# A fused two-block transformer kernel: the pooling stage's bias and banks, a sibling's opening, and products in four gaps

## The reference

```python
for i in range(2):
    f = swiglu(rms_norm(x, g[0]), ffn_w_gate[i, 0], ffn_w_up[i, 0], ffn_w_down[i, 0])   # ffn00, ffn10
    x = x + 0.5 * rms_norm(f, g[1])
    h = rms_norm(x, g[2])
    m = pool_mixer(h, ...) if i == 0 else nsa_mixer(h, ...)                              # pool, nsa
    x = x + rms_norm(m, g[3])
    f = swiglu(rms_norm(x, g[4]), ffn_w_gate[i, 1], ffn_w_up[i, 1], ffn_w_down[i, 1])   # ffn01, ffn11
    x = x + 0.5 * rms_norm(f, g[5])

def pool_mixer(h, w_grp, b_grp, scale):      # group g: trailing mean over 2, 4, 8, 16 tokens minus self
    d = stack([mean_g(h) - h for each of 4 groups of 256 columns])
    return (einsum('bsgc,gce->bsge', d, w_grp) + b_grp).reshape(B, S, D) * scale
```

## Time and profile before

| | |
|---|---|
| time before, median of 3 runs | 2128.64 us (2126.76 to 2135.26) |
| the profiled execution's own time | 2128.28 us |
| its span in the trace | 2126.5 us |
| PE busy | 2050.9 us, 96% of the span |
| DVE busy | 874.7 us, 41% |
| ACT busy | 694.9 us, 33% |
| mean granted TensorE clock | 0.984 of full speed |

### The profile page before, as it was taken

One profiled execution on the slowest core, in us unless ns is written; L12 is line 12 of the kernel. 1 busy time (PEld: TensorE's weight loads), 2 busy tenths in 40 slices (PEclk: granted clock), 3 DMA queues, 4 the chain that ended last, 5 costly groups with the idle time before them and its releaser, 6 DMA issues.

```text
span 2126.5 us, 29241 instructions
## 1 busy us (share of the span) xinstructions
PE 2050.9 (96%) x12345; PEld 1446.3 (68%) x12345; DVE 874.7 (41%) x1244; ACT 694.9 (33%) x966; POOL 16.4 (1%) x30
## 2 busy tenths in 40 slices
PE   8999999999899999999998999899999999899998
PEld 7854444443497444443446999699989988657997
DVE  5831111111376111111116555655575565565555
ACT  5521111111353111111114333433353353454333
POOL 2000000000000000000000000000000000000000
PEclk9999999999999999999999999999999999799999
DMA  8589999999848999999999534545356334505620
GB/s 272 231 374 428 427 429 429 429 429 428 340 159 353 380 427 429 429 429 428 428 428 390 196 127 173 201 155 194 141 216 227 102 129 159 198 1 198 238 99 20
DMA packets 117424, 599.10 MB, mean 282 GB/s; under 512 B 6283, under 2 KB 21867, under 8 KB 92764
## 3 DMA queue, kind: packets, MB, share of 16 engines
q1 hardware_dynamic: 115186, 592.01, 69.5%
q0 software_dynamic: 1888, 5.78, 1.0%
q10 hardware_dynamic: 266, 0.08, 0.0%
HBM read 596.81 MB, written 1.05 MB: 281 GB/s over the span
## 4 chain that ended last, share of the span: by engine, by line
PE 83%; DMA 11%; DVE 4%; ACT 1%; issue 1%; DVEq 0%; ACTq 0%
PE PS L1167 21%; PE PS L1008 16%; PE PS L1181 9%; PE PS L1021 8%; DMA ring<-in_w_expert_up 6%; DMA work<-in_w_expert_up 5%; PE PS L995 4%; PE PS L854 3%; PE PS L1301 2%; PE PS L1154 2%; PE PS L1031 2%; PE PS L906 2%; PE PS L1193 2%; PE PS L1471 1%; PE PS L1048 1%; PE PS L1394 1%
## 5 line engine op out<-in xcount | busy, mean ns | idle before, releaser
L1503 ACT ACTIVATE split<-ring 128x2048 fp32r<-128x2048 f32 x132 | 253.1, 1920 | 410.6 <-PE PS L1167 270.4
L2056 DVE TENSOR_TENSOR split<-ring,split 128x2048 fp32r<-128x2048 f32 x132 | 302.7, 2293 | 170.8 <-ACT split L1503 165.8
L1167 PE MATMUL PS<-hT_high,split 128*128 128x256 f32 x2560 | 329.1, 281 | 0.0
L1167 PEld LDWEIGHTS PS<-hT_high,split 128*128 128x128 f32 x2560 | 316.5, 189 | 2.8
L1008 PE MATMUL PS<-ring,xs 128*64 128x512 f32 x1344 | 301.8, 604 | 12.9 <-DMA ring<-in_w_expert_up 12.9
L1008 PEld LDWEIGHTS PS<-ring,xs 128*64 128x64 f32 x1344 | 99.0, 139 | 209.7 <-issue 198.2
L1021 PE MATMUL PS<-ring,work 128*64 128x512 f32 x672 | 226.6, 595 | 0.0
L1181 PE MATMUL PS<-split,ffn_hid 128*128 128x512 f32 x864 | 202.6, 390 | 0.0
L2319 DVE TENSOR_TENSOR work<-PS,work 128x512 f32<-128x512 f32 x32 | 22.1, 692 | 396.0 <-PE PS L1008 396.0
L1181 PEld LDWEIGHTS PS<-split,ffn_hid 128*128 128x128 f32 x864 | 159.7, 188 | 31.7
L1167 PE MATMUL PS<-hT_low,split 128*128 128x256 f32 x1280 | 178.3, 282 | 0.0
(11 more groups left out here) (333 smaller groups left out, 2140.0 us busy)
## 6 DMA issues: line engine op xcount, KB each, us to landing
ring<-in_w_expert_gate SPq DMA_DIRECT2D x44, 2048.0 KB, 26.0
ring<-in_w_expert_down SPq DMA_DIRECT2D x42, 2048.0 KB, 29.3
ring<-in_w_expert_up SPq DMA_DIRECT2D x40, 2048.0 KB, 26.0
work<-in_w_expert_up SPq DMA_DIRECT2D x24, 2048.0 KB, 26.0
work<-in_w_expert_down SPq DMA_DIRECT2D x22, 2048.0 KB, 27.1
work<-in_w_expert_gate SPq DMA_DIRECT2D x20, 2048.0 KB, 26.4
ring<-in_ffn_w_gate SPq DMA_DIRECT2D x20, 2048.0 KB, 8.7
ring<-in_ffn_w_up SPq DMA_DIRECT2D x20, 2048.0 KB, 9.3
```

The source lines that it names most:

```text
L1167: last = pe.matmul(PS[:, bank, ft * SEQ:(ft + 1) * SEQ], split_cols(b, kind, part)[:, k, ft * P:(ft + 1) * P], hx[:, k, :], start=(n_ == 0 ...
L1503: return act.activation(o, i, ACT.Copy)
L2056: v.tensor_tensor(at[:, 1], src, at[:, 0], ALU.subtract).then_inc(S.w_low, 1)
```

## The change

Three things are changed; the numbers of lines are those of the kernel before.

1. **Pool.** The products of h go into banks 4 to 7 and are taken from there. Right behind them, and ahead of PE's wait for ACT and DVE, four products of one row and 512 columns write the bias into banks 0 to 3 and open them. The eight bias products of 256 columns are gone, and all 16 weight products add to the opened banks.
2. **ffn00's opening.** PE makes the first pass of the up sums between the second and the third pass of the gate sums, and spreads the norm factor behind all 96 products. ACT takes its half of the transposes between its two squares of the raw x, and makes two high parts (up of block 0, gate of block 1) ahead of the squares of the scaled x. DVE makes `hT_low` ahead of scaling x, and the low part of up of block 0 ahead of the norm factor and the diagonal.
3. **Gap products.** In `transpose_x`, between the transposes of token tile 0 and the wait for tile 1, there are 13 filler products in ffn01 and 7 in ffn10, nsa and ffn11, into bank 0.

The other feed-forward stages keep their order: `first_sums` is only written in another way there.

```diff
@@ transpose_x
                         if t and k % 2:
                             last.then_inc(S.hT_psum, 1)
+                    if t == 0 and name in ("ffn01", "ffn10", "nsa", "ffn11"):
+                        keep_clock(13 if name == "ffn01" else 7)
@@ ffn, PE
+                def first_sums():
+
+                    pe.wait_ge(S.w_low, w.to(S.w_low))
+                    one_pass("gate", 0, hT_high, first=True)
+                    one_pass("gate", 1, hT_high)
+                    if name == "ffn00":
+                        pe.wait_ge(S.w_high, w.to(S.w_high, 2))
+                        one_pass("up", 0, hT_high, first=True)
+                        pe.wait_ge(S.hT_low, w.to(S.hT_low))
+                        one_pass("gate", 0, hT_low, last_part=True)
                     else:
+                        pe.wait_ge(S.hT_low, w.to(S.hT_low))
+                        one_pass("gate", 0, hT_low, last_part=True)
+                        spread_r()
                         pe.wait_ge(S.w_high, w.to(S.w_high, 2))
...
+                        one_pass("up", 0, hT_high, first=True)
+                    one_pass("up", 0, hT_low)
+                    pe.wait_ge(S.w_low, w.to(S.w_low))
+                    one_pass("up", 1, hT_high, last_part=True)
+                    if name == "ffn00":
+                        spread_r()
@@ pool_mix, PE
-                        last = pe.matmul(PS[:, c // 2, (c % 2) * SEQ:(c % 2 + 1) * SEQ], hp[:, t, c * P:(c + 1) * P],
+                        last = pe.matmul(PS[:, 4 + c // 2, (c % 2) * SEQ:(c % 2 + 1) * SEQ], hp[:, t, c * P:(c + 1) * P],
                                          means[:, t, c // 2, :], start=(t == 0), stop=(t == 1))
                     if c % 2:
                         last.then_inc(S.hT_psum, 1)
+                for j in range(2 * TT):
+                    pe.matmul(PS[:, j, :], ones[0:1, 0:P], bias[:, (j % 2) * 512:(j % 2 + 1) * 512],
+                              start=True, stop=False, skip_group_check=True)
...
                         for c in range(2):
-                            pe.matmul(o, hT[:, 2 * g + c, t * P:(t + 1) * P], wv[:, 2 * g + c, :],
-                                      start=(c == 0), stop=False)
-                        last = pe.matmul(o, ones[0:1, 0:P], bias[:, g * 256:(g + 1) * 256],
-                                         start=False, stop=True)
+                            last = pe.matmul(o, hT[:, 2 * g + c, t * P:(t + 1) * P], wv[:, 2 * g + c, :],
+                                             start=False, stop=(c == 1), skip_group_check=True)
@@ final, ACT
                     act.wait_ge(S.act_step, w.to(S.act_step))
+                    if t == 0:
+                        take_ffn_hT(FFN_GAIN["ffn00"])
                 roots(root, ss, D, S.root_ready)
-                take_ffn_hT(FFN_GAIN["ffn00"])
+                high("ffn00", 0, "up")
+                high("ffn00", 1, "gate")
...
                 roots(rootc, ssc, D, S.root_ready)
-                high("ffn00", 0, "up")
@@ ffn, DVE
                 w.past(S.hT_odd, 2)
+                v.wait_ge(S.hT_odd, w.after(S.hT_odd, 0))
+                v.wait_ge(S.hT_even, w.after(S.hT_odd, 0))
+                for k in range(KT):
+                    last = v.scalar_tensor_tensor(hT_low[:, k, :], PS[:, 4 + k // 2, (k % 2) * SEQ:(k % 2 + 1) * SEQ],
+                                                  gT[:, gain, k:k + 1], hT_high[:, k, :], ALU.mult, ALU.subtract)
+                last.then_inc(S.hT_low, 1)
                 if name == "ffn00":
                     final_gain = gain_rows()
...
-                v.wait_ge(S.hT_odd, w.after(S.hT_odd, 0))
...
-                last.then_inc(S.hT_low, 1)
+                    low(name, 0, "up")
...
-                low(name, 0, "up")
+                if name != "ffn00":
+                    low(name, 0, "up")
```

More of the change, by code:

```diff
@@ L787, in transpose_h, with keep_clock @@
                 pe.wait_ge(S.hT_odd, w.to(S.hT_odd, 2))
+            def keep_clock(n_, bank=0):
+                for _ in range(n_):
+                    pe.matmul(PS[:, bank, :].rearrange("p (s k) -> p s k", s=4), ident_r[:, :],
+                              ident_r[:, :].unsqueeze(1).to_broadcast([P, 4, P]), start=True, stop=True)
             def transpose_x(name, bank):
@@ L1085, in experts @@
                 return past_more
-            def keep_clock(n_, bank=0):
-                for _ in range(n_):
-                    pe.matmul(PS[:, bank, :].rearrange("p (s k) -> p s k", s=4), ident_r[:, :],
-                              ident_r[:, :].unsqueeze(1).to_broadcast([P, 4, P]), start=True, stop=True)
             def moe(l):
@@ L1135, in split_cols, with one_pass @@
                     return split[:, buffer_of(b, kind), part, :].rearrange("p (k n) -> p k n", k=KT)
-                def first_sums(kind):
-                    gate = kind == "gate"
-                    if gate:
-                        pe.wait_ge(S.w_low, w.to(S.w_low))
-                    else:
+                def one_pass(kind, part, hx, first=False, last_part=False):
+                    for k in range(KT):
+                        if kind == "gate" and first and k % 2 == 0:
+                            odd = (k // 2) % 2
+                            pe.wait_ge(S.hT_odd if odd else S.hT_even, w.to(S.hT_odd if odd else S.hT_even))
+                        for ft in range(2):
+                            last = pe.matmul(PS[:, 2 * (kind == "up") + ft, 0:SEQ],
+                                             split_cols(0, kind, part)[:, k, ft * P:(ft + 1) * P], hx[:, k, :],
+                                             start=(first and k == 0), stop=(last_part and k == KT - 1))
+                    if last_part:
+                        last.then_inc(S.ffn_used, 1)
@@ L1143, in first_sums @@
                         pe.wait_ge(S.w_high, w.to(S.w_high, 2))
-                    for n_, (part, hx) in enumerate(products() if gate else ((0, hT_high), (0, hT_low), (1, hT_high))):
-                        if gate and n_ == 2:
-                            pe.wait_ge(S.hT_low, w.to(S.hT_low))
-                        if not gate and n_ == 2:
-                            pe.wait_ge(S.w_low, w.to(S.w_low))
-                        for k in range(KT):
-                            if gate and n_ == 0 and k % 2 == 0:
-                                odd = (k // 2) % 2
-                                pe.wait_ge(S.hT_odd if odd else S.hT_even, w.to(S.hT_odd if odd else S.hT_even))
-                            for ft in range(2):
-                                last = pe.matmul(PS[:, 2 * (kind == "up") + ft, 0:SEQ],
-                                                 split_cols(0, kind, part)[:, k, ft * P:(ft + 1) * P], hx[:, k, :],
-                                                 start=(n_ == 0 and k == 0), stop=(n_ == 2 and k == KT - 1))
@@ L1211, in ffn @@
                 transpose_x(name, 4)
-                first_sums("gate")
-                pe.wait_ge(S.diag_made, w.to(S.diag_made))
-                for t in range(TT):
-                    last = pe.matmul(PS[:, 4, t * P:(t + 1) * P], ones, FB.sF[:, t, 0:P], start=True, stop=True)
-                last.then_inc(S.r_wide, 1)
-                first_sums("up")
+                first_sums()
                 wide_sums(1, "gate")
@@ L1794, in follow @@
                     high(name, b, "down")
-                high(name, 1, "gate")
+                if name != "ffn00":
+                    high(name, 1, "gate")
                 follow(0)
@@ L2463, in ffn @@
                     w.past(S.x_ready, TT)
-                v.wait_ge(S.hT_odd, w.after(S.hT_odd, 0))
-                v.wait_ge(S.hT_even, w.after(S.hT_odd, 0))
-                for k in range(KT):
-                    last = v.scalar_tensor_tensor(hT_low[:, k, :], PS[:, 4 + k // 2, (k % 2) * SEQ:(k % 2 + 1) * SEQ],
-                                                  gT[:, gain, k:k + 1], hT_high[:, k, :], ALU.mult, ALU.subtract)
-                last.then_inc(S.hT_low, 1)
+                    low(name, 0, "up")
                 v.wait_ge(S.root_ready, w.to(S.root_ready))
```

12 lines of the change are left out of this document (9 added, 3 removed).

## The result

| | median | runs | lowest to highest |
|---|---|---|---|
| before | 2131.75 us | 20 | 2124.81 to 2135.31 |
| after | 2123.48 us | 20 | 2118.09 to 2129.08 |

The ratio is 0.9972, with a 95% interval of 0.9965 to 0.9979. That is 6.0 us less, between 4.5 and 7.5, where I had forecast 9.4 (0.9955). The two medians of the table lie 8.3 us apart and the means 7.0; I go by the ratio on record, which has the interval. The change is well clear of zero and under the 0.5% bound. The profiled execution after took 2122.55 us with a span of 2120.8, against 2128.28 and 2126.5.

The account below looks back on a forecast made before the run. PE was taken as the bound from ffn00 on, through idle time, slow-clock products and products that can be left out. 2.4 + 3.0 + 4.0 = 9.4 us gave 2119.0 us, ratio 0.9955, range 2112.5 to 2125.

Parts of the forecast that it names:

- ffn00, 2.4 us forecast: ffn00's opening: reordered work lets block 1 start at 1153.6 in place of 1156.02; gain 2.4 us, bounds 1.9 and 2.9.
- The gap products, 4.0 us forecast: Fillers keep the clock full behind four gaps: 1.65 (ffn01), 0.8 (ffn10), 0.55 (ffn11), 1.0 us (nsa); bounds 0 and 4.6.
- The pool, 3.0 us forecast: Pool: bias products in one piece ahead, DVE's two tile chains without a hole; gain 3.0 us, bounds 2.4 and 3.3.
- rival B: Pool: one-row bias openings lower the clock, tile 0 comes 1.7 to 3.4 us later; 2120.7 to 2122.4 us; chance 0.09.
- The switches: Pool: two switches between 128 rows and one cost 0.4 us per group; afterwards one at either end of the bias products.
- rival A: The clock inside nsa falls elsewhere: down to 2114 to 2117 us, chance 0.18; up to 2122 to 2123, chance 0.14.
- My own sign of being wrong: In nsa: a change of its length by more than 2 us would show the prediction wrong.
- rival C: The gap products do not hold the clock, only 2.4 + 3.0 us remain: 2123.2 us; chance 0.07.

Follow-up runs that it names:

- openings of 128 rows: The changed kernel with its four openings made with 128 rows instead of one, columns of the matrix of means in place of the bias; ratio to before 0.9960.
- fillers ahead of h: The changed kernel with 16 filler products added in PE's idle time ahead of h; one time, 2123.58 us.
- pool alone: The kernel before with only the pool's part of the change (banks, four wide one-row openings, weight products adding to them); ratio to before 0.9999.
- early openings: The changed kernel with its one-row openings moved into PE's idle time ahead of h, in two pairs; ratio to before 0.9956.

## Why the prediction was wrong in the pool, and where it was right

- **ffn00, 2.4 us forecast, 2.46 measured.** Right by its own steps: DVE's work was permuted without a hole, its low part of gate 1 is the releaser, and no new wait came behind. In four more kernels it was 2.48.
- **The gap products, 4.0 us forecast.** 1.70, 0.87 and 0.61 in the three feed-forward stages, and in nsa the product behind its first 48 starts 12.43 us after the second transposes in place of 13.50, 1.07: together 4.25. DVE's hT_low took the bound over with a wait of 0.2 us, as I had it. But the 4.0 was priced from one execution, in which the clock happened to be slow behind all four gaps. Over the three profiles without fillers the mean is 2.0 us, and the kernel with the fillers alone gained 2.3 (-0.2 to 4.7). That the term came out between these two traces is in part luck.
- **The pool, 3.0 us forecast, 1.7 lost (+4.10 and -2.38).** This is the step that failed: "16 weight products stream in 6.8 us, and the four bias products ... in 3.4 us", all at the full clock. That DVE's two chains would follow each other without a hole was right: 4.36 us apart, and the 2.38 is exactly that. But tile 0 came 4.7 us later than forecast. h itself, which nobody touched, ran at 1.2 GHz for longer, about 1.2 us, and that part is not the change's; the openings took 1.2 us more than their stream; tile 0's eight weight products took 5.8 us in place of 3.4. With openings of 128 rows the same step came out, at 3.3 us. I gave this mechanism, rival B, 0.09, and priced it at 1.7 to 3.4 us on the weight products alone, leaving out the openings' own slow end.
- **Why I weighed B so low.** The row that I held against it was that one-row products had taken a quarter of a stretch at full clock. The other three quarters were 128-row products, so that row says nothing of one-row products alone. The wrong inference was to read a mixture as evidence for its smaller part.
- **The switches.** With one-row openings behind h there are two switches in place of 16. Up to the first weight product the two cost 0.3 us at full clock ("fillers ahead of h" against 128 rows), where the kernel before lost 0.4 us in each of its eight groups; the forecast had this right. By the Trainium skill, "TensorE: Matmul & The Clock Gate", Part 2, weight loads are pulled ahead of matmuls in flight when the row groups don't conflict or when the load goes to the background weight buffer. With 128 rows throughout the trace agrees: the load of the first weight product starts at 1344.58, together with the last opening, and 0.43 us ahead of its product. Behind a one-row opening at full clock it starts at 1349.41, together with its product and 0.52 us after that opening; why a change of rows holds it back stays open.

```profile
1344.58 0.19 PEld L1276 LDWEIGHTS PS<-ring,hT 128*128 128x128 f32 x1 [0.24 <-issue]
```

```profile
1349.41 8.46 PEld L1277 LDWEIGHTS PS<-ring,hT 128*128 128x128 f32 x32 [0.76 <-issue]
```
- **nsa, rival A.** Its slow stretches did move: the stage lost 2.63 us, of which 1.07 is its opening, so 1.6 us is theirs. It pointed downwards, as the larger of A's two chances had it, but smaller than its price. Without it the result would have been smaller still. My own sign of being wrong, a change of nsa's length by more than 2 us, came true. The stretches after, where the earlier trace rows had 0.55 over 15 us and 0.52 over 14:

```profile
1808.00:1822.00 14.00, 10.22 (x65) 8.09 (x66) 9.79 (x28) 6.46 (x20) 0.00 (x0) 0.76 0.26 105
1832.50:1848.50 16.00, 14.46 (x74) 12.08 (x74) 9.96 (x27) 6.10 (x23) 0.00 (x0) 0.57 1.04 396
```
- **The total.** 0.62 lay on a change within 0.5%, and the ratio is within it, but its interval excludes no change. By the traces the gain was 3.7 us short of the 9.4: the pool's 4.7 and 0.8 of drift ahead of the change, less 1.6 from nsa and 0.3 from ffn00 and the fillers (rounded). So the total owes part of its closeness to falls of the clock in nsa that the forecast didn't count. It is also luck that the median, 2123.48, stands beside rival C's 2123.2: C had the fillers fail, and they held in every profile.

## What to carry to other kernels

Count a matmul's rows before using it to fill PE's time: a product of one row streams as long as one of 128, and here its stretch left the clock at half for the dense work behind it. If a bias has to open a bank, do it in idle time that exists anyway, and with all rows. To price a small edit in a long program, compare distances between fixed points of two traces; the total carries the drift of every stage before. But one trace shows one execution's falls of the clock: price what a steady clock is worth from several.

## What the runs showed of the hardware

- Four one-row products in a row, 3.4 us of uninterrupted busy PE, took the granted clock from 1.00 to 0.50 in every profile that had them behind h (after, pool alone, fillers ahead of h); the same columns with 128 rows left it at 1.00. In the idle time ahead of h it went the same way, as counted under the early openings. The Trainium skill, "TensorE: Matmul & The Clock Gate", Part 1, says that the clock follows how busy the PE has been recently. Here "busy" can't be what the profile's busy time shows: PE was 2.00 of 2.00 us busy in the stretch where it fell in "pool alone".
- Between kernels whose program is the same up to there, ffn00's second transposes came anywhere from 1137.64 us (early openings) to 1144.09 (fillers ahead of h). That drift of 6.5 us lies ahead of everything that was changed, and is as large as the effect; the 193.6 us of ffn00 behind it repeated to 0.02 us in the five kernels with the new opening and nothing added ahead of h.
- In the four kernels with the pool as before, tile 0 was taken 17.08 to 18.21 us after the first product of h, though from the last product of h it was 8.3 us in all four: after the idle time ahead of h the clock came back sooner or later.
- Behind the gaps of 2.2 to 3.5 us ahead of the second transposes, the products ran partly at half clock in 7 of 12 cases without fillers (three profiles) and in 0 of 44 with fillers (eleven profiles).
